# Two heads' value products in alternate column halves, a second buffer for their transposed probabilities, and a third projection step of 396 columns

## The reference, cut to what matters

```python
z = rms_norm_2(x, norm_mix_pre[l]) @ w_in[l]
za, zq, zkv, zg, zc, zd = jnp.split(z, offsets, axis=-1)     # 512, 256, 384, 12, 512, 256 columns
y_conv = conformer_conv(za, ...)                             # 31 taps along the tokens, layer norm, silu
y_nsa  = nsa_attention(q, kv..., gates, ...)                 # 4 heads of 64, three branches:
#   g0 * softmax(q kc) vc  +  g1 * softmax(qr ks) vs  +  g2 * softmax(qr kw) vw
y_sgu  = spatial_gating(zc, ...)                             # gelu, layer norm, a 128x128 product over tokens
y_pool = multiscale_pool(zd, ...)
x = x + rms_norm_2(concat([y_conv, y_nsa, y_sgu, y_pool]) @ w_out[l], norm_mix_post[l])
```

## Time and profile before

| | |
|---|---|
| median of 3 runs | 1902.08 us (1899.97 to 1904.26) |
| span of the profiled execution | 1901.7 us (the three runs' median is 0.4 us above it) |
| PE busy | 1805.5 us, 95% |
| DVE busy | 1466.5 us, 77% |
| ACT busy | 1049.8 us, 55% |
| data read | 379.90 MB, 200 GB/s over the span |
| mean granted TensorE clock | 0.980 of full |

### The profile page before, as it was taken

How to read it: one execution, slowest core, us unless ns; L and a number is a source line. 1 busy time by engine, 2 the same in 40 slices (tenths; PEclk the granted TensorE clock), 3 DMA queues, 4 the chain that set the end, 5 groups by cost and what they waited for, 6 DMA issues and landing times.

```text
span 1901.7 us, 28364 instructions
## 1 busy us (share of the span) xinstructions
PE 1805.5 (95%) x9730; PEld 1512.8 (80%) x9730; DVE 1466.5 (77%) x2300; ACT 1049.8 (55%) x1594; POOL 131.0 (7%) x170
## 2 busy tenths in 40 slices
PE   5999899899999999999999999999889998979998
PEld 4888677688888887788878798878678887768886
DVE  6888788688888888868665576658869976878994
ACT  5554465465536553555454465545676645666663
POOL 1101010000010000000000000000012200002210
PEclk9999999899999999999999999999999999999999
DMA  9878665367888777444540164545145554324553
GB/s 384 339 274 313 236 232 210 113 220 277 279 305 287 276 278 271 165 179 176 180 151 1 64 243 176 194 177 193 67 180 191 184 194 160 112 89 169 185 193 117
DMA packets 63778, 382.04 MB, mean 201 GB/s; under 512 B 7153, under 2 KB 7409, under 8 KB 27586
## 3 DMA queue, kind: packets, MB, share of 16 engines
q1 hardware_dynamic: 42912, 300.96, 43.9%
q0 software_dynamic: 20208, 78.79, 11.5%
q10 hardware_dynamic: 578, 1.22, 0.2%
HBM read 379.90 MB, written 1.05 MB: 200 GB/s over the span
## 4 chain that ended last, share of the span: by engine, by line
PE 74%; DVE 14%; issue 6%; ACT 4%; DVEq 1%; DMA 1%; SPq 0%; ACTq 0%
PE ps L561 18%; PE ps L478 11%; PE ps L480 10%; PE ps L479 10%; PE ps L563 9%; DVE ring_lo L1615 3%; DVE wb L1914 2%; PE ps L843 1%; PE ps L582 1%; PE ps L584 1%; PE ps L583 1%; PE ps L609 1%; PE ps L869 1%; DVE wa L1903 1%; PE ps L856 1%
## 5 line engine op out<-in xcount | busy, mean ns | idle before, releaser
L1615 DVE TENSOR_TENSOR ring_lo<-ring,w_hi 128x1024 fp32r<-128x1024 f32 x534 | 666.5, 1265 | 257.5 <-ACT w_hi L1137 255.8
L1137 ACT ACTIVATE w_hi<-ring 128x1024 fp32r<-128x1024 f32 x556 | 579.1, 1057 | 458.7 <-PE ps L480 282.2
L561 PE MATMUL ps<-h_both,w_hi 128*128 128x512 f32 x1984 | 698.5, 397 | 0.0
L563 PE MATMUL ps<-h_both,ring_lo 128*128 128x256 f32 x1984 | 557.3, 281 | 0.0
L561 PEld LDWEIGHTS ps<-h_both,w_hi 128*128 128x128 f32 x1984 | 373.1, 188 | 89.0
L563 PEld LDWEIGHTS ps<-h_both,ring_lo 128*128 128x128 f32 x1984 | 375.8, 189 | 0.0
L478 PE MATMUL ps<-w_hi,h_both 128*128 128x512 f32 x580 | 236.8, 408 | 12.5 <-DVE h_both L2099 6.4
L480 PE MATMUL ps<-w_hi,h_both 128*128 128x512 f32 x580 | 230.2, 397 | 0.0
L479 PE MATMUL ps<-ring_lo,h_both 128*128 128x512 f32 x580 | 230.1, 397 | 0.0
L478 PE MATMUL ps<-w_hi,hid_lo 128*128 128x512 f32 x456 | 180.3, 395 | 1.3 <-DVE ring_lo L1615 1.3
L480 PE MATMUL ps<-w_hi,hid_hi 128*128 128x512 f32 x456 | 177.6, 389 | 0.0
(11 more groups left out here) (362 smaller groups left out, 2161.7 us busy)
## 6 DMA issues: line engine op xcount, KB each, us to landing
ring<-in_stream SPq DMA_DIRECT2D x276, 1024.0 KB, 4.8
arena<-in_mod POOLq DMA_DIRECT2D x128, 512.0 KB, 5.6
arena<-in_mod SPq DMA_DIRECT2D x14, 512.0 KB, 13.4
gate<-in_wide POOLq DMA_DIRECT2D x3, 1536.0 KB, 10.3
arena<-in_nsaw POOLq DMA_DIRECT2D x2, 1072.0 KB, 8.7
ring<-in_stream SPq DMA_DIRECT2D x4, 512.0 KB, 14.9
arena<-in_konst POOLq DMA_DIRECT2D x1, 1295.5 KB, 8.4
arena<-in_mixw POOLq DMA_DIRECT2D x2, 576.0 KB, 9.6
```

What stands on the lines that cost most here:

```text
L561: nc.tensor.matmul(ps[:, banks[b], :].rearrange("p (w t) -> p w t", w=2), hi, h_both[:, :, 2 * r + i, :], start=(r == 0 and i == 0), stop= ...
L563: mm = nc.tensor.matmul(ps[:, banks[b], T:2 * T], lo, h_hi[:, 2 * r + i, :], start=False, stop=(r == 3 and i == 1))
L1137: nc.scalar.activation(w_hi[:, q % SPLITS, :], ring[:, half % SLOTS, (q % 2) * QUARTER:(q % 2 + 1) * QUARTER], ACT.Copy).then_inc(w_hi_rea ...
L1615: v.tensor_tensor(ring_lo[:, slot, cs], ring[:, slot, cs], w_hi[:, q % SPLITS, :], ALU.subtract).then_inc(w_lo_ready, 1)
```

## The change

Three things change. In the third projection step the matmuls stream 396 columns (`MIX_COLS`) and leave the zero columns out. `nsaT` becomes two buffers, one for even and one for odd heads. And `values` now takes a pair of heads: their matmuls stand alternately in the two column halves. The pair of heads 0 and 1 stands after `gating()`, the pair of heads 2 and 3 after `out_chunk(2)`.

```diff
+MIX_COLS = (512, 512, 396, 512)
...
-        nsaT = hidT[:, 4508:5532]
+        nsaT = [hidT[:, 4508:5532], arena[:, a0 + MIX_W + NS1 + NS0:a0 + MIX_W + NS1 + NS0 + 1024]]
...
-                    quarter(q0 + 4 * j + r, None, 0, lhs, lambda i, tt: ps[:, bank + tt, :],
-                            lambda i: r == 0 and i == 0, lambda i: r == 3 and i == 1)
+                    n = MIX_COLS[j]
+                    quarter(q0 + 4 * j + r, None, 0, lhs, lambda i, tt: ps[:, bank + tt, 0:n],
+                            lambda i: r == 0 and i == 0, lambda i: r == 3 and i == 1, wide=n)
...
-                def values(h):
-                    i = NH * l + h
-                    pe.wait_ge(npT_copied, i + 1)
+                def values(pair):
+                    pe.wait_ge(npT_copied, NH * l + 2 * pair + 2)
+                    heads = (2 * pair, 2 * pair + 1)
                     vs = lambda w, tile: dv[:, tile, C2 + w * HD:C2 + (w + 1) * HD]
-                    dst = ps[h % 2 * HD:(h % 2 + 1) * HD, 7, h // 2 * T:(h // 2 + 1) * T]
+                    dst = [ps[h % 2 * HD:(h % 2 + 1) * HD, 7, pair * T:(pair + 1) * T] for h in heads]
                     for w in range(2):
-                        nc.tensor.matmul(dst, vs(w, 0), nsaT[:, w * FW:w * FW + T], start=(w == 0), stop=False)
-                        nc.tensor.matmul(dst[:, P:T], vs(w, 1), nsaT[:, w * FW + T:(w + 1) * FW], start=False, stop=False)
-                    nc.tensor.matmul(dst, vc, nsaT[0:NCMP, 6 * P:8 * P], start=False, stop=True).then_inc(no_sum, 1)
+                        for h in range(2):
+                            nc.tensor.matmul(dst[h], vs(w, 0), nsaT[h][:, w * FW:w * FW + T], start=(w == 0), stop=False)
+                        for h in range(2):
+                            nc.tensor.matmul(dst[h][:, P:T], vs(w, 1), nsaT[h][:, w * FW + T:(w + 1) * FW], start=False, stop=False)
+                    for h in range(2):
+                        nc.tensor.matmul(dst[h], vc, nsaT[h][0:NCMP, 6 * P:8 * P], start=False, stop=True).then_inc(no_sum, 1)
...
                 out_chunk(0)
-                values(0)
                 turn_probs(1)
                 out_chunk(1)
-                values(1)
                 turn_probs(2)
                 gating()
-                values(2)
+                values(0)
                 turn_gating()
                 turn_probs(3)
                 pe.wait_ge(sgu_out, l + 1)
                 out_chunk(2)
-                values(3)
+                values(1)
...
                 def take_probs(h):
                     i = NH * l + h
                     dve.wait_ge(np_T, i + 1)
-                    if h >= 1:
-                        dve.wait_ge(no_sum, i)
-                    v.tensor_copy(nsaT[:, 0:768], psf[:, bA * 512:bA * 512 + 768])
-                    v.tensor_copy(nsaT[0:NCMP, 768:1024], ps[0:NCMP, bA + 1, C2:512]).then_inc(npT_copied, 1)
+                    if h >= 2:
+                        dve.wait_ge(no_sum, NH * l + 2)
+                    v.tensor_copy(nsaT[h % 2][:, 0:768], psf[:, bA * 512:bA * 512 + 768])
+                    v.tensor_copy(nsaT[h % 2][0:NCMP, 768:1024], ps[0:NCMP, bA + 1, C2:512]).then_inc(npT_copied, 1)
```

More of the change, by code:

```diff
@@ L290, in build @@
         mixw = arena[:, a0:a0 + MIX_W]
-        assert a0 + MIX_W + 2 * T + 2 * P + 2 * NCMP <= ARENA, a0
+        assert a0 + MIX_W + 2 * T + 2 * P + 2 * NCMP + 1024 <= ARENA, a0
         hidT = arena
@@ L466, in low_part, with quarter @@
                     pe.wait_ge(w_lo_ready, val(it, q + 1 - before, per - mine))
-            def quarter(q, it, per, lhs, out_of, first, last, ends=False):
+            def quarter(q, it, per, lhs, out_of, first, last, ends=False, wide=512):
                 low_part(q, it, per)
@@ L473, in quarter @@
                 for n, (i, tt) in enumerate(order):
-                    hi = w_hi[:, buf, i * 512:(i + 1) * 512]
-                    lo = ring_lo[:, slot, half + i * 512:half + (i + 1) * 512]
+                    hi = w_hi[:, buf, i * 512:i * 512 + wide]
+                    lo = ring_lo[:, slot, half + i * 512:half + i * 512 + wide]
                     x_hi, x_lo = lhs(i, tt)
```

## The result

| | before | changed |
|---|---|---|
| median, 17 runs each | 1902.39 us (1899.61 to 1905.63) | 1912.82 us (1903.74 to 1916.93) |
| ratio, 95% interval | | 1.0049 [1.0040, 1.0058] |
| span of the profiled execution | 1901.7 us | 1911.9 us |
| its mean granted clock | 0.980 | 0.972 |

The changed kernel is slower: by 0.49% by the ratio, by 10.4 us between the medians. The forecast was 1903.1 us, with a range that ended at 1907.5.

A forecast was written before the change was run, and what follows sets the result against it. PE's time was taken as the bound, but among the output chunks a chain through PE, DVE and ACT. 1901.7 - 4.6 + 4.0 + 1.6 = 1902.7, with 0.4 to the median 1903.1 us; range 1898.0 to 1907.5.

The forecast's parts named there:

- The clock, +1.6: PE's clock among the output chunks: one fall before, up to four now; -1.6 to +4.8 us, middle +1.6 taken.
- falls at all four places: Rival: the clock falls at all four idle places, costing 4.8 instead of 1.6 us, 1906.3 us; chance 0.15.
- The step, -4.6: Third projection step: 48 matmuls a layer, each 116 columns shorter, save 2.3 us a layer, -4.6 in all.
- The halves side by side, 2.0 us a pair: Value products: two heads run side by side in the column halves, 2.0 us a pair, 4.0 apart.
- the prediction's count of passes: Rival of program order alone: a pair takes ten 256-column passes instead of eight, +1.7 us in all, 1904.8; chance 0.08.
- The chain, +4.0: Output chunks: DVE's copy for head 2 waits for the pair, gated product 2.0 us later a layer, +4.0.
- The covered copy, 1896.7: Rival: DVE's copy for head 2 does not delay gating; 1.2 us a layer gained, not 2.0 lost; chance 0.12.
- four signs given for a wrong prediction: Profile: DVE still waiting for gating; pair of 3 us or more; maxima not ended by PE; clock 1.00 throughout.

The follow-up runs named there:

- e2: The changed kernel with 512 columns in the third projection step, so the new arrangement of the value products alone: 1917.58 us, ratio 1.0076.
- e5: The changed kernel with unread products of 256 columns in all four idle places among the output chunks: 1901.69 us, ratio 0.9998.
- e3: The changed kernel with four buffers for the transposed probabilities, one a head, so head 2's copy waits for no value product: 1897.68 us, ratio 0.9977.
- e12: The changed kernel with four buffers and unread products (8, 0, 2, 3), plus four more ahead of the first transposes: 1894.49 us, ratio 0.9956.
- e6: The changed kernel with four buffers and unread products in the idle places left (8, 0, 2, 3): 1897.34 us, ratio 0.9975.
- e1: The kernel before with the third projection step at 396 columns and nothing else: 1901.62 us, ratio 0.9999.
- e9: The kernel before with the narrower third step and unread products in its idle places among the chunks: 1896.99 us, ratio 0.9965.

## Why the prediction was wrong

- **The clock, +1.6.** This term failed. It measured +10.0, and its ceiling of 3 x 1.6 = 4.8 was as wrong as the middle. The places were named rightly; the size was not. I took a fall's price from the one row where a slow stretch met the third chunk, 1.6 us, as if each fall touched one chunk and ended. But a fall lies over whatever PE does until the clock comes back: `turn_probs(2)`, gating, pair, `turn_gating`, `turn_probs(3)`, chunk, all on the path. 17 us at half clock on this chain cost 5.6 us in the first mixer, and 20 us in the second cost 5.9: about 0.3 us for each. (A further 3.4 us at half clock in the second mixer's first chunk cost nothing: `turn_probs(2)` came 12.2 us behind `turn_probs(0)` in both mixers, since it waits for ACT.) The rows to price it by stood in the prediction: gating's 1.83, the pair's 2.0, `turn_probs(2)` 0.93. At half clock each takes that much more: 4.8 us a mixer at most, before the third chunk and its 1.6.
- **The rival "falls at all four places"** came nearest to the mechanism, at 0.15 and with half the price. It was not right in its count either: in the first mixer the clock fell at both places, in the second only at the first and stayed down over the other. Against it I held that the second mixer kept full clock after 3.78 busy of 6.3 us. In the changed kernel single stretches without any matmul are 3.85 and 2.51 us long, where the longest in that row is 1.71, so the row spoke of another case.
- **The step, -4.6.** Right in size. 0.183 us apart for the 0.178 expected, `compress` 2.2 us sooner against the norm ahead of the mixer (2.3 expected), -4.3 up to `turn_probs(0)`, 5.1 between e2 and the changed kernel. How the -3.0 and -1.3 divide between step and clock isn't shown: in the first mixer before had 6.8 us at half clock on that way and the changed kernel none, in the second 7.6 and 11.3. DVE's slack was used up, the 2.48 us of rows 4 and one more wait of 0.21 at 1331.40 that the reading left out: the first maxima come 3.0 us sooner against the norm, now without any wait.

```profile
1332.60 0.41 DVE L2217 CUSTOM_DVE_ANT_0 arena<-ps,arena 128x256 f32<-128x256 f32 x1
```

- **The halves side by side, 2.0 us a pair.** Right: 2.03 and 2.04 at full clock. The rule of the Trainium skill (TensorE: Matmul & The Clock Gate, The mechanism), that matmuls start and end in program order, would have made it 2.43 by the prediction's count of passes, an estimate. The traces do not agree, neither nor the pair's 2.03.
- **The chain, +4.0.** Right: 2.1 a mixer at full clock, with the wait, the order and the gated product as described. ACT's wait ahead of head 3 grew to 8.67 us and not to 5.3; in e5, at full clock, it is 5.42.
- **The covered copy, 1896.7.** Not this kernel, but e3 built it, and e12 with fills: 1897.7 and 1894.5.

Two of the four signs given for a wrong prediction came. The first pair takes 3.1 us, and 3 or more was to speak against the sum; it came by half the clock, and not by halves that don't run side by side. And the first maxima are no longer ended by PE. The other two asked for a faster kernel, and none asked for a gating of over 1.83 us.

What stays open: why e6 gains nothing over e3, though its trace is 2.7 us shorter; why the clock falls within `compress` in before and e1 and not in the changed kernel and e9; and why e1 shows no gain. Its 7 us more at half clock than before, at 0.3 each, would explain about half of the missing 4.4, and the rest is about as large as what its interval leaves open, 2 us to either side.

## What to carry to other kernels

Work that is taken from TensorE between waits on the path can cost time: list what it does after each new idle stretch until the next dense one, and count all of it a second time, at half clock, as the most that a fall can cost, before you book the gain. Where idling can't be removed, products that nobody reads, sized to end before the wait does, are worth a trial. Put a merged product where its buffers don't hold up the engine that feeds the path; here two more buffers turned +0.5% into -0.2%.

## What was unexpected of the hardware

- Added useless products made the kernel 9.7 us faster (ratio 1.0049 to 0.9998).
- Once at 1.2 GHz, TensorE stayed there for 20.4 us (1671.2 to 1691.6) while it did small products between waits and then most of a dense chunk. In the first mixer it was back after 6.8 us, and fell again 3.4 us later.
- The clock can fall where PE's rows leave no gap: 3.3 us into `compress` before and 2.7 us into it in e1, among 128 passes of 15 columns. In e9 and in the changed kernel the same passes ran at full clock.
- Two products in different column halves overlap: 2.03 us for two heads, 2.01 for one alone. In `pooled()` they do so although the program writes both products of one half ahead of those of the other.
- An fp32 product of 512 columns is two passes of 0.44 us each (7.03 us for sixteen), where the rounded parts in the projections take 0.226 us for the same columns.
